# Three recurrence jobs made inside the recurrence projection; compression's gathers, weights and tables made inside the attention projection, its prompt unit first

## The chip, the cores and the metric

The kernel runs on one core of one Trainium2 chip. A core has five engines that run side by side: TensorE (PE in the profile) multiplies matrices into PSUM, VectorE (DVE) and ScalarE (ACT) do elementwise work, GpSimd (POOL) does elementwise work and issues indexed transfers, SyncE (SP) issues plain transfers. They meet by semaphores. The metric is the device time of one execution in microseconds (us); the time given is a median of runs.

## The reference, cut to what matters

One inference step of a hybrid decoder layer, for a prompt of 1024 rows and 8 sample sequences of one new row each (their 2048 past rows lie in pages). Two parts of it are touched. The first is the compression of raw keys and values, in chunks of 16 rows, for the 8 sequences (gathered by the page table) and for the prompt:

```
parts = jnp.einsum('bnsgd,rsdh->rbngh', ch, w1r)          # ch: chunks of 16 rows; r: first or second half of a block
h = parts[0, :, 0:n_cmp] + parts[1, :, 1:1 + n_cmp] + (pe.reshape(-1) @ w1) + b1
out = jax.nn.gelu(h) @ w2 + b2                            # once for keys, once for values
```

The second is a gated recurrence with 4 heads, in exact chunkwise form:

```
b = jnp.cumsum(gc, axis=2)                                # log decays
decay = jnp.exp(jnp.where(tri, b[:, :, :, None, :] - b[:, :, None, :, :], -jnp.inf))
att = jnp.einsum('bhtk,bhtsk,bhsk->bhts', qc, decay, kc)
s = jnp.exp(b_end)[..., None] * s + jnp.einsum('bhsk,bhsv->bhkv', kc * jnp.exp(b_end[:, :, None, :] - b), vc)
```

Around them stand LayerNorm and modulation, one input projection (in pieces), three attention branches, the merge, an output projection and a convolutional feed-forward. All products are float32, many as three passes over high and low parts.

## The kernel before, in words

The program is a row of stages, each a block of its own with a barrier of all engines between: modulation and norm, `project_attention` (L609), `compress` (L738), `decode_attention`, `prompt_attention`, `project_hgrn` (L1804), `hgrn_and_merge` (L1965), output projection, feed-forward. The order inside a stage is written out by hand for each engine. Nothing of a later stage starts before the barrier.

`project_attention` makes 39 products (events) from five 256-column pieces of the input weights; ACT reads the even events out of PSUM and DVE the odd ones. POOL and SP have little to do in it: SP loads the last weights at L647 and then stores the raw keys and values (L654 to L665).

`compress` first loads the page table and small constants (L821 to L831) and the first-layer weights for keys (L833), makes row indices from the page table (L905, L1092), and gathers 1 MB of pages for each sequence (L854). It works in ten units: for keys and then for values, four units of two sequences and, last of the five, one prompt unit, which reloads the prompt's rows from the stored output (L852). Per unit: 32 transposes (L899; 16 for the prompt), copied out of PSUM by ACT and DVE (L1008, 512 columns a piece); a difference on POOL (L867) and one on DVE (L1112); the first layer for two halves of the hidden units, three groups of 8 products each (L947, L949, L954, of 256 columns or of 64 for the prompt), the third group with a sum of weights that POOL makes (L874); GELU; the second layer (L969 for keys, L974 for values). A float32 product leaves two records in the trace, so a group of 8 is x16. In the eight sequence units one slice of the late modulation is worked in beside: `late_rows` (L919) between the two halves, an ACT copy (L1057), and `late_back` (L926) right behind the first layer. The transposes of unit u+1 stand before the first layer of unit u. Behind the units come the transposes and scores of the selection keys (L899, L1003).

`project_hgrn` makes 54 events from nine pieces; the last two pieces (units 7 and 8, 9 events each) only give the recurrence's inputs, and DVE makes the running sums of the log decays beside them (L1962). `hgrn_and_merge` runs 9 jobs for each of 4 heads. Jobs 0 to 6 are levels of a binary splitting: DVE makes differences of log decays (L2388, L2389; job 0 has its own form on ACT, L2296 and L2297), ACT the exponential (L2304), POOL one half of the product with k (L2105) and DVE the other with q (L2401), PE the products (L2185, L2192), DVE picks them out by a mask (L2418). Job 7 is a plain exponential, job 8 the decay to the chunk's end: a DVE difference (L2393), an exponential, a POOL product. The buffers for decays and for products are rings of three, so three jobs can be ahead.

Of the kernel before, what the change touches and what calls it, by code (L numbers as in the profile page):

```python
# [16 lines left out]
ALU = mybir.AluOpType  # L17
ACT = mybir.ActivationFunctionType
AX = mybir.AxisListType
F32 = mybir.dt.float32  # L20
# [94 lines left out]
def build(nc, a, o):  # L115
# [21 lines left out]
    with ExitStack() as ctx:  # L137
# [15 lines left out]
        with ExitStack() as left:  # L153
            with ExitStack() as att:
                with ExitStack() as h:
                    m["hTh"] = sb(h, "h_hi_1", [P, KD, T])
                    m["hTl"] = sb(h, "h_lo_1", [P, KD, T])
                    m["hl"] = [m["hTl"][:, k, :] for k in range(KD)]
                    w0, wide = nc.sbuf_base + 4 * KD * 512, 2 * GD + 3 * HEADS
                    m["w_att"] = SplitWeights(nc, None, sem, "w_att", wide, (  # L160
                        nc.alloc_sbuf_tensor_at("w_att_raw", [P, 2, 4, wide], F32, offset=w0),
                        nc.alloc_sbuf_tensor_at("w_att_parts", [P, 2, 2, KD, wide], F32, offset=w0 + 4 * 8 * wide)))
                    m["pa_mm"] = sem("pa_mm_done")
                    modulation_and_norm(nc, a, o, m, PS, sem)
                    m["kv"] = sb(att, "kv", [P, NT + 1, 6 * GD + 3 * HEADS], side="right")
                    m["qT"] = sb(att, "qT", [P, 4, T], side="right")
                    m["ksT"] = sb(att, "ksT", [P, T], side="right")
                    m["kwT"] = sb(att, "kwT", [P, T], side="right")
                    m["bg"] = sb(att, "bg", [P, NT + 1, 3 * HEADS], side="right")
                    project_attention(nc, a, o, m, PS, sem)  # L170
                m["kcTp"] = sb(att, "kcTp", [P, P], side="right")
                m["vcp"] = sb(att, "vcp", [P, GD], side="right")
                with ExitStack() as dec:
                    m["kcT"] = sb(dec, "kcT", [P, NB, NCD], side="right")
                    m["vc"] = sb(dec, "vc", [P, NB, GD], side="right")
                    m["Qz"] = sb(dec, "Qz", [P, NB * 72], side="right")
                    m["Qd"] = sb(dec, "Qd", [P, NB * HEADS], side="right")
                    m["rows"] = sb(dec, "cache_rows", [P, NB], I32, side="right")
# [13 lines left out]
            with hg:  # L192
# [13 lines left out]
                m["hl"] = [m["h_low0"][:, :]] + [m["h_low"][:, k, :] for k in range(1, KD)]  # L206
                project_hgrn(nc, a, o, m, PS, sem, at, nc.alloc_sbuf_tensor_at("scan_keep", [P, P], F32, offset=low_at))
                m["hl"] = [m["h_low"][:, k, :] for k in range(KD)]
                m["nref"] = nc.alloc_sbuf_tensor_at("minus_middle", [P, HH, NT], F32, offset=low_at + 1024)
# [399 lines left out]
def project_attention(nc, a, o, m, PS, sem):  # L609
# [4 lines left out]
    even_read, odd_read, kT_done, kT_read, stored = (sem("pa_" + x) for x in ("even_read", "odd_read", "kT_done", "kT_read", "stored"))  # L614
    with ExitStack() as st:
# [14 lines left out]
        KVQ = 3 * (NT + 1)  # L630
        block = st.enter_context(nc.Block())

        @block.sync
        def _(sp):
            sp.dma_start(m["h_hi_dram"][:, :, :], m["hTh"][:, :, :]).then_inc(spilled, 16)
            sp.dma_start(m["h_lo_dram"][:, :, :], m["hTl"][:, :, :]).then_inc(spilled, 16)
            for u, (z0, cols) in enumerate(units):
                if u < 2:
                    continue
                for s in range(2):  # L640
# [7 lines left out]
                    else:  # L648
                        sp.dma_start(weights.raw[:, s, :, 0:cols], w_dram[:, 4 * s:4 * s + 4, z0:z0 + cols]).then_inc(weights.raw_in[s], 16)
            sp.wait_ge(even_read, (KVQ + 1) // 2)  # L650
# [21 lines left out]
        def _(pe):  # L672
            unit = 0
            for e in range(FIRST, NEV):
                u, left, right, rows, cols = events[e]
                if u != unit:
                    unit = u
                    weights.ready(pe, u)
                if e >= 8:
                    pe.wait_ge(odd_read if e % 2 else even_read, e // 2 - 3)  # L680
                product(pe, PS[0:rows, EVENT_BANK[e % 8], 0:cols], left, right, KD).then_inc(mm_done, 1)

            pe.wait_ge(even_read, (NEV + 1) // 2)
            pe.wait_ge(odd_read, len(events) // 2)
# [2685 lines left out]
```

## Time and profile before

| what | value |
|---|---|
| median of 3 runs (lowest, highest) | 2432.14 us (2424.17, 2436.47) |
| the profiled execution: its own time, its span | 2429.2 us, 2427.4 us |
| mean granted TensorE clock of it | 0.954 of full |
| busy PE, DVE, ACT, POOL | 92%, 40%, 28%, 29% of the span |

The profile cuts the span into 40 slices of 60.7 us. `compress` lies in slices 4 to 9 (188 to 540 us), the recurrence in slices 19 to 21 (1092 to 1216 us). The granted clock has two levels in the records, 1.0 (2.4 GHz) and 0.5 (1.2 GHz); a value between is a mean over a stretch with both. In a timeline row the columns are start, duration, engine, line, operation, out<-in with shapes, how many instructions are merged, and in brackets the idle time before them with what ended it.

### The profile page before, as it was taken

How to read it: one execution, taken by the hardware profiler on the slowest of the kernel's cores; microseconds unless marked ns; L12 is line 12 of the kernel's file. 1: busy time of each engine (PE TensorE's matmuls, PEld its weight loads, DVE VectorE, ACT ScalarE, POOL GpSimd, SP SyncE). 2: the span in 40 equal slices, each digit the busy share in tenths (PEclk: the TensorE clock that was granted, in tenths of full speed). 3: DMA queues.
4: the chain of work that ended last, by engine and by line, in shares of the span. 5: the costliest groups of instructions: out<-in, count | busy, mean ns of one | idle time of the engine just before them, and what ended most of it. 6: DMA issues, size and time to landing. Idle time of an engine off the chain costs nothing. (4 is left out here: it accounts for less than half of the span.)

```text
span 2427.4 us, 35781 instructions
## 1 busy us (share of the span) xinstructions
PE 2236.0 (92%) x14938; PEld 1973.8 (81%) x14938; DVE 962.3 (40%) x1860; ACT 675.1 (28%) x1402; POOL 713.2 (29%) x424
## 2 busy tenths in 40 slices
PE   5996999997899989996799999999999999999997
PEld 3995777863667769995798999678989899898996
DVE  5104333123566650229932035665323333223227
ACT  3102222112465641225522221233212121121213
POOL 3203222110111122205521214264424242341526
PEclk9997999976899999997899999999999999999998
DMA  6536343226200013100032130323201120110202
GB/s 245 186 122 234 120 145 130 86 90 219 112 30 30 10 43 106 53 1 8 21 90 87 53 104 19 99 72 133 67 28 53 38 68 27 53 53 27 79 18 89
DMA packets 137655, 197.00 MB, mean 81 GB/s; under 512 B 15233, under 2 KB 106299, under 8 KB 132766
## 3 DMA queue, kind: packets, MB, share of 16 engines
q1 hardware_dynamic: 129083, 150.33, 19.3%
q0 software_dynamic: 8368, 44.12, 5.2%
q8 instruction: 118, 1.93, 0.3%
q14 instruction: 42, 0.34, 0.1%
q10 hardware_dynamic: 44, 0.27, 0.0%
HBM read 172.61 MB, written 26.36 MB: 82 GB/s over the span
## 5 line engine op out<-in xcount | busy, mean ns | idle before, releaser
L3062 PE MATMUL PS<-part_hi,w_ff_hi 128*128 128x344 f32 x1024 | 329.0, 321 | 0.0
L3062 PE MATMUL PS<-part_hi,w_ff_lo 128*128 128x344 f32 x1024 | 326.9, 319 | 0.0
L3062 PE MATMUL PS<-part_lo,w_ff_hi 128*128 128x344 f32 x1024 | 326.7, 319 | 0.0
L3062 PEld LDWEIGHTS PS<-part_hi,w_ff_hi 128*128 128x128 f32 x1024 | 192.5, 188 | 5.5 <-issue 5.1
L3062 PEld LDWEIGHTS PS<-part_lo,w_ff_hi 128*128 128x128 f32 x1024 | 192.2, 188 | 0.3
L3062 PEld LDWEIGHTS PS<-part_hi,w_ff_lo 128*128 128x128 f32 x1024 | 192.4, 188 | 0.0
L3186 POOL TENSOR_TENSOR w_ff_lo<-w_raw,w_ff_hi 128x1024 fp32r<-128x1024 f32 x42 | 100.8, 2399 | 283.5 <-ACT w_ff_hi L3139 283.5
L3239 DVE TENSOR_SCALAR conv_sb<-up_sb,conv_wT 128x1024 f32<-128x1024 f32 x22 | 44.0, 1999 | 279.6 <-ACT up_dec L3153 279.6
L1696 ACT ACTIVATE scores<-scores,mins_p 128x640 f32<-128x640 f32 (+5 forms) x192 | 112.9, 590 | 121.4 <-DVE mins_p L1736 121.4
L3103 PE MATMUL PS<-w_down_hi,act_hi 128*128 128x512 f32 x352 | 139.7, 397 | 0.0
L3103 PE MATMUL PS<-w_down_lo,act_hi 128*128 128x512 f32 x352 | 138.7, 394 | 0.0
L3103 PE MATMUL PS<-w_down_hi,act_lo 128*128 128x512 f32 x352 | 138.5, 394 | 0.0
L2160 PE MATMUL PS<-h_hi,w_merge_parts 128*128 128x344 f32 x768 | 132.2, 324 | 0.0
L3263 DVE TENSOR_TENSOR y_sum<-y_sum,PS 128x512 f32<-128x512 f32 x112 | 76.2, 687 | 138.5 <-PE PS L3103 138.2
L2160 PEld LDWEIGHTS PS<-h_hi,w_merge_parts 128*128 128x128 f32 x768 | 122.8, 189 | 3.1 <-issue 3.0
L568 POOL TENSOR_TENSOR w_merge_parts<-w_merge_raw,w_merge_parts 128x1024 fp32r<-128x1024 f32 x24 | 59.6, 2509 | 204.1 <-ACT w_merge_parts L561 204.1
L580 PE MATMUL PS<-h_hi,w_hg_parts 128*128 128x344 f32 x480 | 113.8, 320 | 0.0
L3181 POOL TENSOR_TENSOR w_down_lo<-w_down_scaled,w_down_hi 128x1024 fp32r<-128x1024 f32 x22 | 53.8, 2446 | 157.6 <-ACT w_down_hi L3134 157.6
L3139 ACT ACTIVATE w_ff_hi<-w_raw 128x1024 fp32r<-128x1024 f32 x42 | 44.5, 1058 | 194.2 <-PE PS L3062 191.2
L3134 ACT ACTIVATE w_down_hi<-w_down_scaled 128x1024 fp32r<-128x1024 f32 x22 | 23.3, 1061 | 259.4 <-PE PS L3103 193.0
L580 PE MATMUL PS<-h_hi,w_merge_parts 128*128 128x344 f32 x384 | 91.1, 320 | 1.6 <-DVE part_lo L2501 1.6
L1640 PE MATMUL PS<-ident,scores 128*128 128x128 f32 x592 | 82.5, 282 | 7.3 <-ACT PT L1691 5.6
(519 smaller groups left out, 4965.5 us busy)
## 6 DMA issues: line engine op xcount, KB each, us to landing
w_or_ada<-w_ada SPq DMA_DIRECT2D x8, 2048.0 KB, 7.9
w_raw<-w_up SPq DMA_DIRECT2D x22, 512.0 KB, 4.9
w_raw<-w_gate SPq DMA_DIRECT2D x22, 512.0 KB, 4.1
w_raw<-w_down SPq DMA_DIRECT2D x22, 512.0 KB, 3.6
w_ada_sb<-w_ada SPq DMA_DIRECT2D x4, 2048.0 KB, 17.7
w_merge_raw<-w_in SPq DMA_DIRECT2D x16, 512.0 KB, 3.9
w_hg_raw<-w_in SPq DMA_DIRECT2D x14, 512.0 KB, 3.6
h_hi_rows<-h_hi SPq DMA_DIRECT2D x1, 4128.0 KB, 13.4
```

Of the source, the lines that this page charges most:

```text
L568: pool.tensor_tensor(r32(self.lo[:, u % 2, k, 0:cols]), self.raw[:, s, :, 0:cols], self.hi[:, u % 2, k, 0:cols], ALU.subtract).then_inc(se ...
L580: last = pe.matmul(out, r32(x), r32(y), start=k + i == 0, stop=k == tiles - 1 and i == 2)
L1640: last = pe.transpose(PS[:, 4 + G % 3, P * k:P * k + P], S[:, n % 2, g, at:at + P], ident[:, :])
L1696: act.activation(S[:, n % 2, g, c:c + cols], S[:, n % 2, g, c:c + cols], ACT.Exp, bias=mn[:, n % 2, x, g:g + 1], scale=-1.0, accum_out=sm[ ...
L2160: last = pe.matmul(PS[:, e % RING, 0:W3], r32(left), r32(right), start=p == 0 and k == 0, stop=p == 2 and k == KD - 1)
L3062: last = pe.matmul(PS[:, bank(e), 0:cols], r(wt[:, s, k, :]), r(ht[:, k, t0:t0 + cols]), start=k + i == 0, stop=k == KD - 1 and i == 2)
L3103: last = pe.matmul(PS[:, bank(e), :], r(at_[:, f % AR, P * t:P * t + P]), r(wt[:, f % GRP, c]), start=f == fs[0] and i == 0, stop=f == fs[ ...
L3139: act.activation(r(wgh[:, int(kind == "gate"), :, :]), raw[:, n % RAW, :].rearrange("p (k n) -> p k n", k=KD), ACT.Copy).then_inc(hi_done, 1)
L3181: pool.tensor_tensor(r(wdl[:, f % GRP, :]), wds[:, :], wdh[:, f % GRP, :], ALU.subtract).then_inc(lo_done, 1)
L3186: pool.tensor_tensor(r(l_), w, h, ALU.subtract).then_inc(lo_done, 1)
L3239: own(v.tensor_scalar(c, up[:, 0:L], taps[0], taps[3], ALU.mult, ALU.add))
L3263: v.tensor_tensor(d, d, s, ALU.add).then_inc(acc_read, 1)
```

## The change

Three edits in one. (1) `project_attention` now also issues, on SP behind its last weights, the loads of the page table, the small constants and the keys' first-layer weights; PE makes the index product and two small transposes in a spare corner of the banks of events 29 and 31; POOL clears four tiles, makes the weight sum and issues the gathers of three sequences. Buffers get fixed places for it. (2) In `compress` the prompt unit is the first of each five, and its transposes read the projected rows `kv` in SBUF (8 transposes, 4 copies of 256 columns for a group) and not a reload. `late_rows` stands before the first half of a unit (before the second in the first sequence unit of keys and of values), and `late_back` behind the second layer of the unit before. (3) `project_hgrn` makes jobs 0, 1 and 2 of the recurrence up to their products, in the shadow of its last unit; and in all four heads job 8's difference on DVE and its one exponential become eight exponentials on ACT with the chunk's last column as bias.

```
@@ project_attention
             for u in range(1, len(units)):
                 weights.low(pool, u, landed(u), units[u][1])
+            for x in ("kcTp", "vcp", "Qz", "Qd"):
+                pool.memset(m[x][:, :], 0.0)
+            pool.wait_ge(cp["w1_in0"], 16)
+            w1 = cp["w1_or_ada0"]
+            pool.tensor_tensor(cp["w1_sum"][:, :, :], w1[:, 0:8, :], w1[:, 8:16, :], ALU.add).then_inc(sum_ready, 1)
+            pool.wait_ge(idx_ready, 2)
+            pool.wait_ge(weights.lo_done, 2 * len(units))
...
+            for b in range(3):
+                if b == 1:
+                    pool.wait_ge(mm_done, ends[3])
+                pool.indirect_dma_start(cp[f"raw{b}"][:, :], None, pages, bass.IndirectOffsetOnAxis(m["rows"][:, b:b + 1], 0))\
+                    .then_inc(cp[f"raw_in{b}"], 16)
...
+                if e == IDX:
+                    pe.wait_ge(idx_ready, 1)
+                    pe.matmul(spare(e, P, 0, NB), part[:, :], ptF[:, :], start=True, stop=True)
@@ compress
+        for pr in (None,) + tuple(range(NB // 2)):
...
+            if n is None:
+                z = GD * units[u][0]
+                for q in range(2):
+                    bank_free(pe, base + q)
+                    for t in range(4):
+                        last = pe.transpose(PS[:, (base + q) % 3, P * t:P * t + P], kv[:, 4 * q + t, z:z + GD], ident[:, :])
+                    last.then_inc(tr_done, 1)
+                return
...
-                pe.wait_ge(hb_ready, n // (len(LATE) // 2) + 1)
...
-                    if hh and u in late_at:
+                    if u in late_at and hh == late_half(u):
                         late_rows(late_at.index(u))
...
-                if u in late_at:
-                    late_back(late_at.index(u))
...
                 if u:
                     layer2(u - 1)
+                if u in late_at:
+                    late_back(late_at.index(u))
@@ project_hgrn, scalar
+                        if e in (ends[LAST - 1] + 3, ends[LAST - 1] + 5):
+                            J = (e - ends[LAST - 1] - 1) // 2
+                            act.wait_ge(diff_done, J)
+                            act.activation(E[:, J, :], E[:, J, :], ACT.Exp).then_inc(exp_done, 1)
...
+                if u == LAST - 1:
+                    raw_over(act)
+                    act.wait_ge(nref_ready, 1)
+                    first_decays(act, E, lf, nref, 0).then_inc(exp_done, 1)
@@ project_hgrn, gpsimd
+            for J in range(3):
+                pool.wait_ge(exp_done, J + 1)
+                parts_over(pool)
+                pool.tensor_tensor(pair_halves(X[:, J], J)[0], pair_halves(E[:, J], J)[0], pair_halves(kk[:, 0, 0:L], J)[0], ALU.mult)\
+                    .then_inc(mul_done, 1)
@@ hgrn_and_merge, scalar
+                elif w == 8:
+                    products_done(act, J - 3)
                     for c in range(NT):
+                        n, end = P * c, P * c + P - 1
+                        last = act.activation(E[:, J % 3, n:n + P], lf[:, h, n:n + P], ACT.Exp, bias=lf[:, h, end:end + 1], scale=-1.0)
                     last.then_inc(exp_done, 1)
```

On PE, at the start of `compress` (`kv` are the projected rows, `raw` the gathered pages, `XT` the transposed chunks), before:

```order
L905 MATMUL PS<-ptF,pagepart 128x8
L907 MATMUL PS<-ident,pe_rows 128x32
L908 MATMUL PS<-ident,b_rows 128x4
L899 MATMUL PS<-ident,raw 128x128 x64
L947 MATMUL PS<-XT,w_or_ada 128x257 x8
L949 MATMUL PS<-XT,w_or_ada 128x253 x8
L954 MATMUL PS<-XT,w_sum 128x256 x8
L919 MATMUL PS<-w_or_ada,cT 32x512 x8
```

and now:

```order
L941 MATMUL PS<-ident,kv 128x128 x8
L950 MATMUL PS<-ident,raw_570 128x128 x16
L950 MATMUL PS<-ident,raw_571 128x128 x16
L991 MATMUL PS<-XT,w_or_ada_569 128x65 x8
L993 MATMUL PS<-XT,w_or_ada_569 128x63 x8
L998 MATMUL PS<-XT,w_sum 128x64 x8
```

The index product and the small transposes are gone from here, the first first-layer groups have 64 columns and not 256, and 40 transposes stand before them instead of 64.

On DVE, at the end of `project_hgrn` and the start of the recurrence (`decays` is the ring of differences, `X` that of products), before:

```order
L1943 COPY iv<-PS 8x256
L1811 UNCONDITIONAL_BRANCH
L2375 UNCONDITIONAL_BRANCH
L2433 TENSOR_SCALAR minus_middle<-q_k_logf 128x32
L2388 TENSOR_TENSOR decays<-q_k_logf 128x16x32
L2389 TENSOR_TENSOR decays<-q_k_logf 128x16x32
L2401 TENSOR_TENSOR X<-decays,q_k_logf 128x8x64
L2388 TENSOR_TENSOR decays<-q_k_logf 128x32x16
L2389 TENSOR_TENSOR decays<-q_k_logf 128x32x16
L2401 TENSOR_TENSOR X<-decays,q_k_logf 128x16x32
L2388 TENSOR_TENSOR decays<-q_k_logf 128x64x8
```

and now:

```order
L2008 COPY iv<-PS 128x256
L2041 TENSOR_TENSOR X<-decays,q_k_logf 128x8x64
L2008 COPY iv<-PS 128x256
L2041 TENSOR_TENSOR X<-decays,q_k_logf 128x16x32
L2008 COPY iv<-PS 8x256
L2041 TENSOR_TENSOR X<-decays,q_k_logf 128x32x16
L1845 UNCONDITIONAL_BRANCH
L2464 UNCONDITIONAL_BRANCH
L2474 TENSOR_TENSOR decays<-q_k_logf 128x64x8
L2475 TENSOR_TENSOR decays<-q_k_logf 128x64x8
```

Behind the barrier (the two branches) DVE now begins with job 3's difference; one multiplication of job 2 stands between the last PSUM copy and the barrier.

## Rows read from the trace of the kernel before

**Rows 1.** Stretches: busy time of each engine, clock, DMA share and GB/s.
```profile
192.00:203.00 11.00, 0.96 (x4) 0.78 (x4) 2.34 (x13) 0.00 (x0) 4.00 (x4) 0.50 0.55 193
203.00:209.00 6.00, 5.96 (x27) 5.64 (x28) 3.12 (x5) 3.59 (x6) 1.63 (x2) 0.50 1.03 415
209.00:213.00 4.00, 3.13 (x23) 2.21 (x21) 3.91 (x7) 3.17 (x6) 3.84 (x3) 0.99 1.02 396
346.00:357.00 11.00, 11.00 (x101) 10.93 (x100) 7.39 (x9) 1.58 (x5) 4.72 (x3) 1.00 0.49 180
484.00:507.00 23.00, 23.00 (x110) 23.00 (x109) 1.07 (x5) 1.25 (x4) 0.00 (x0) 0.50 0.00 1
1100.00:1200.00 100.00, 73.04 (x839) 68.46 (x838) 96.81 (x110) 51.68 (x133) 52.70 (x32) 0.74 0.04 13
```
**Rows 2.** Timeline at the start of the compression.
```profile
187.97 0.28 PE L692 MATMUL PS<-ident,kv 8*128 8x8 f32 x2
195.34 1.15 POOL L854 DMA_INDIRECT raw<-cache_cmp_k,cache_rows  x1 [48.82 <-DVE cache_rows L1092]
203.04 6.73 PE L899 MATMUL PS<-ident,raw 128*128 128x128 f32 x32 [3.72 <-DMA raw<-cache_cmp_k,cache_rows]
205.12 1.39 DVE L1008 COPY XT<-PS 64x512 f32<-64x512 f32 x2 [5.51 <-PE PS L899]
220.86 4.51 POOL L874 TENSOR_TENSOR w_sum<-w_or_ada 128x2048 f32<-128x2048 f32 x1 [6.75 <-DMA w_or_ada<-cmp_w]
221.34 4.33 PE L947 MATMUL PS<-XT,w_or_ada 128*128 128x257 f32 x16
235.08 2.40 PE L919 MATMUL PS<-w_or_ada,cT 128*32 128x512 f32 x16 [2.53 <-DVE hid_bias L1124]
```
**Rows 3.** Timeline, PE, one sequence unit of keys to the next.
```profile
256.25 3.63 PE L947 MATMUL PS<-XT,w_or_ada 128*128 128x256 f32 x16
280.08 1.06 PE L926 MATMUL PS<-groupsum,ada_rows_late 128*128 128x9 f32 x8 [0.96 <-ACT ada_rows_late L1057]
287.30 3.63 PE L947 MATMUL PS<-XT,w_or_ada 128*128 128x256 f32 x16
```
**Rows 4.** Timeline, PE, the two prompt units and around them.
```profile
346.06 1.90 PE L947 MATMUL PS<-XT,w_or_ada 128*128 128x64 f32 x16
363.05 3.64 PE L947 MATMUL PS<-XT,w_or_ada 128*128 128x257 f32 x16
454.46 5.58 PE L947 MATMUL PS<-XT,w_or_ada 128*128 128x256 f32 x16
483.69 3.62 PE L947 MATMUL PS<-XT,w_or_ada 128*128 128x64 f32 x16
507.59 4.89 PE L899 MATMUL PS<-ident,raw 128*128 128x128 f32 x32
```
**Rows 5.** Timeline of the attention projection, SP's queue and POOL.
```profile
100.88 23.10 SPq L647 DMA_DIRECT2D w_att_raw<-w_in  x32
141.77 4.75 POOL L568 TENSOR_TENSOR w_att_parts<-w_att_raw,w_att_parts 128x1024 fp32r<-128x1024 f32 x2 [23.53 <-ACT w_att_parts L561]
```
**Rows 6.** Timeline at the start of the recurrence, DVE.
```profile
1091.60 0.41 DVE L1943 COPY iv<-PS 8x256 f32<-8x256 f32 x1 [5.22 <-PE PS L580]
1092.43 0.84 DVE L2388 TENSOR_TENSOR decays<-q_k_logf 128x512 f32<-128x512 f32 x1
1108.11 1.29 DVE L2418 COPY_PREDICATED att<-levels,PS 128x1024 f32<-128x1024 int32 x1
```
**Rows 7.** Timeline at a head's end in the recurrence, DVE and ACT.
```profile
1148.43 1.94 DVE L2393 TENSOR_TENSOR decays<-q_k_logf 128x1024 f32<-128x1024 f32 x1
1150.41 1.06 ACT L2304 ACTIVATE decays<-decays 128x1024 f32<-128x1024 f32 x1 [2.49 <-DVE decays L2393]
1155.81 1.80 DVE L2401 TENSOR_TENSOR X<-decays,q_k_logf 128x512 f32<-128x512 f32 x1 [0.77 <-issue]
```
**Rows 8.** Groups by line: count, busy us, mean ns.
```profile
L2296 ACT ACTIVATE decays<-q_k_logf 128x64 f32<-128x64 f32 x32 | 10.7, 334 | 0.0
```

More of the change, by code:

```diff
@@ L747, in compress @@
     caches = [a[x][0].rearrange("n (c s) g d -> (n c) (s g d)", s=STRIDE) for x in ("cache_cmp_k", "cache_cmp_v", "cache_sel_k")]
-    loads, units = [], []
+    loads, units, items = [], [], []
+    group = 0
     for which in range(2):
-        for pr in range(NB // 2):
-            units.append((which, pr, (len(loads), len(loads) + 1)))
-            loads += [(which, 2 * pr), (which, 2 * pr + 1)]
-        units.append((which, None, (len(loads),)))
-        loads.append((which, None))
-    NU, SEL0 = len(units), len(loads)
+        for pr in (None,) + tuple(range(NB // 2)):
+            mine = []
+            for b in ((None,) if pr is None else (2 * pr, 2 * pr + 1)):
+                mine.append(len(items))
+                items.append((len(units), len(mine) - 1, None if b is None else len(loads), group))
+                group += 2 if b is None else 4
+                if b is not None:
+                    loads.append((which, b))
+            units.append((which, pr, tuple(mine)))
@@ L792, in compress @@
-        arow = sb("ada_rows_late", [P, 512])
-        late_at = [u for u in range(NU) if u % (NU // 2) != NU // 2 - 1]
+        raw = [cp[f"raw{i}"] for i in range(RING)]
+        X, wsum, m2, w2, H, peT, b1T, hb, hb0, b2k, b2v, arow = (cp[x] for x in (
+            "XT", "w1_sum", "middle", "w2", "H", "peT", "b1T", "hid_bias", "hid_bias_half", "b2k", "b2v", "ada_rows_late"))
+        wbuf = [cp["w1_or_ada0"], cp["w1_or_ada1"]]
+        late_at = [u for u in range(NU) if units[u][1] is not None]
@@ L803, in shape, with read_to @@
             return (1, NCP + 1, NCP) if units[u][1] is None else (2, CH, NCD)
-        def unit_of(n):
-            return next(u for u in range(NU) if n in units[u][2])
         def evens(u):
             return X[:, u % 2, 0], shape(u)[1] // 2
+        def read_to(it):
+            return (it[3] + (2 if it[2] is None else 4)) // 2
         def odds(u):
@@ L876, in _ @@
[L876 to L888 removed]
+            load(RING - 1)
@@ new lines, in _ @@
+            for it in items + sel:
+                u, _, n, base = it
+                if n is not None and n + RING < len(loads):
+                    pool.wait_ge(tr_done, base + 4)
+                    load(n + RING)
+                if u is not None:
+                    later_difference(it)
+                if u == FIRST[1]:
+                    pool.wait_ge(w_in[1], 16)
+                    pool.wait_ge(l1_done, 2 * (NU // 2))
+                    pool.tensor_tensor(wsum[:, :, :], wbuf[1][:, 0:8, :], wbuf[1][:, 8:16, :], ALU.add).then_inc(sum_ready, 1)
@@ L1062, in _ @@
             u = 0
-            for n in read_chunks(act, 0, even_read):
-                if u + 1 < NU and n == units[u + 1][2][-1]:
+            for k in read_chunks(act, 0, even_read):
+                if u + 1 < NU and k == units[u + 1][2][-1]:
                     gelu(u)
@@ L1154, in late @@
                                     bT[:, t0:t0 + 4, None].to_broadcast([P, 4, 9]), ALU.add).then_inc(wa_added, 1)
[L1156 to L1158 removed]
+            for k in read_chunks(v, 1, odd_read):
+                u = items[k][0]
+                if k == units[u][2][-1]:
                     if u in FIRST:
```

393 lines of the change are left out of this document (202 added, 191 removed).

## The prediction, made before the changed kernel ran

> **What bounds the kernel now.** I read the page first (PE busy 92%), then the stretches where PE is not full or its granted clock is 0.5, then the timelines of the two stages that the change touches. TensorE bounds nearly all of the kernel. Two of its holes are touched here. In the compression's first 33.1 us, from the last small transposes of the attention projection (187.97 + 0.28 = 188.25 us) to the first 257-column group (221.34), PE does only transposes. Read the releasers: the row indices come at 195 us, the pages keep PE until 203.04, and the keys' weights, 2 MB behind everything else at over 400 GB/s, land only at 220.8, where POOL's weight sum starts [rows 1, 2]. After this PE waits once more, 2.53 us, for the hidden bias [rows 2]. In the recurrence DVE is busy 96.8 of 100 us and PE 73 [rows 1]: there DVE is the bound, and what leaves DVE counts.
>
> **Compression, its start.** The dependency on transfers goes. SP issued its last attention weights between 100.88 and 124 us; the twelve new loads stand right behind, and POOL's last weights are done at 146.5 [rows 5]. Before, the whole chain from table to first gather took 7.1 us behind 188.25 [rows 2]; issued at 124 it is through by about 132, some 15 us ahead of event 29. POOL then has the clears and a sum of 4.51 us [rows 2], and gathers from about 153 us and, for the second and third, from about 164, when the values of unit 3 are free. In the first start the first pages took 7.7 us from issue (195.34 to 203.04) [rows 2]; here they have 20. I cost this part at nothing, hidden by PE's own matmuls; if that cover failed, event 29 would stand for the landing of the table, at most these 7 us. PE gets an index product and two small transposes in the middle of its stream: 0.7 us on the path.
>
> What is late next is the reading of PSUM. From the barrier (189.7) DVE has two pairs of small copies (0.8), the prompt's four half-size copies (1.39 is two copies of 512 columns; four of 256 take that or a little more: 1.4 to 1.7), the bias columns, a wait for POOL's small difference (1.3), its own small one (0.7), and then four group reads of 1.39 for the first sequence unit [rows 2]. That is 0.8 + 1.1 (first transposes) + 1.7 + 0.4 + 1.3 + 0.7 + 5.6, so the last of the 32 transposes goes at about 199. PE's first real group therefore starts at 199 and not at 221.34.
>
> **The clock decides what this group costs.** A prompt unit is six groups of 64 columns. At the full level such a group starts every 1.8 us (346.06, 1.90 long: 10.8 us in all), at the half level every 3.42 (483.69, 3.62 long: 20.5 us) [rows 4]. The records show both: full in 346 to 357, half throughout 484 to 507, where 23 us of this work never brought the clock back [rows 1]. So such a unit keeps the level that it finds. It was at 0.5 from 192 us, and came back at 209, after 6 us of transposes at 99% busy [rows 1]. In the changed kernel the transposes are paced by DVE, 28 of them in some 6.5 us where 27 records before filled 6 us, with gaps between. I take the half level, 20.5 us; full would give 9.7 back.
>
> One rule of the Trainium skill bears on it: the page "TensorE: Matmul & The Clock Gate", section "Part 4: PE-mode transpose", says that transposes do not count as busy for the clock in the way matmuls do. This trace disagrees in part: at 209 the clock rose with nothing but transposes before it [rows 1]. By the rule the half level would hold until the first 256-column groups and cost about 1 us more than my sum; the sum goes by the rows.
>
> Then the readers turn to the next unit only when the first layer is through, with GELU of the prompt unit before ACT's read: 5.2 us of transposes and 0.8: the first sequence unit's first layer starts at 199 + 20.5 + 6.0 = 225.5.
>
> **Compression, from there.** One sequence unit of keys takes 31.05 us (256.25 to 287.30), of which 0.96 is PE waiting for ACT's copy before L926 [rows 3]. `late_back` behind the second layer has this copy long finished: 30.1. Eight such are 240.8. The third has the values' prompt transposes (8, not 32) behind it: -4.2; the last two have none there: -10.4; the second layer of values is 1.25 longer in three: +3.7; the prompt's is shorter: -0.8; the values' prompt unit, at the full level as at 346, +17.0 (346.06 to 363.05) [rows 4]. Sum 246.1, so the selection's transposes start at 225.5 + 246.1 = 471.6. Before they started at 507.59 [rows 4]: 36.0 earlier. Behind them the values' second layer of a sequence unit stands in place of a prompt's: +1.6, against transposes at the full clock instead of the half one at 507: -0.8. With the 0.7 above and 1 to 2 us for the clock falling once more in the values' units: **33 us** gained. Where it comes from: the 33.1 us hole becomes 11, the waits at L926 give 7.7, that for the bias 2.5, slow ramps the rest; the prompt unit at half clock is paid before at the end and then at the start, and cancels.
>
> Moved with it: the late modulation's weights now have to be there before a unit's first half. From the second half of one unit to the first of the next there are 30.1 - 10.4 = 19.7 us, and 2 MB at the 415 GB/s of the rows need about 5 [rows 1]. The values' weights leave after the fourth unit's `late_rows` and their sum starts when the keys' first layers are through; PE has 32 transposes and two groups ahead of its use, 9 us against 4.51 [rows 2]. Both at nothing.
>
> **Recurrence.** Before, DVE finished its last copy at 1092.0, began the differences at 1092.43, and reached the first pick (job 2) at 1108.11 [rows 6]. Now it has before this pick only job 3's and job 4's differences and job 3's multiplication: 1.3 to 2.2, 1.3 to 1.7 and 0.7 (the longer ones beside POOL). The barrier comes 0.7 later, for job 2's multiplication behind the last copy. So the pick is at 1093.0 + 4.6 = 1097.7, 10.4 us earlier; the mask (0.4 MB, 1 us at the rate of [rows 1] and some latency) is loaded at the block's start. The added work in the last projection unit (DVE some 7 us, ACT 6, POOL 4, in 26 us where both read only an event of 0.4 us every 5.8) is at nothing: PE's last eight events need no bank back.
>
> Job 8: DVE loses 1.94 in each of four heads [rows 7]. But the next step is not DVE's alone. PE runs almost without a gap there, and the multiplication of the next job 0 (1155.81) waited 0.77 for ACT. ACT now has eight pieces of 128 columns; from 0.334 for 64 columns [rows 8] and 1.06 for 1024 [rows 7] a piece is about 0.38, or 0.29 from start to start: 2.4 in place of 1.06, but it starts about 2.3 earlier. That frees ACT 0.8 to 1.0 sooner. Bounds: nothing (ACT or PE binds), or 4 x 1.94 = 7.8. I take 3.6, near the ACT row. Recurrence: 10.4 + 3.6 = **14 us**.
>
> **Sum.** 33 + 14 = 47 off 2429.2 (span 2427.4 and 1.8 around it): 2382. That execution was 2.9 under the median, so on the median's scale: **2385 us**.
>
> **Rivals.**
> - The clock is at the full level when the first prompt unit starts: 9.7 more off, 2375. For it: forty transposes before it, and in 209 to 213 transposes held the level with PE 78% busy [rows 1]. Against: it falls at 192 in the records, and rose only after 6 us of nearly unbroken transposes.
> - Part of it is given back: the values' prompt unit falls to half (+9.7), ACT's eight pieces eat the job 8 gain (+3.6), the clock falls in further units (3 each): 2398, about 34 us gained. For it: 484 to 507; against: 346 to 357 held [rows 1].
> - It does not do what it says: pages or weights still late, for instance raw pages waited for at each unit, and the recurrence bound by PE at half clock (0.74 mean in 1100 to 1200 [rows 1]): the 33 us hole reopens by 25 and the 14 shrink to 6: 2425 and up, no change.
> - Slower: the clock stays at half after the prompt unit, through sequence units. A group of 256 columns at the half level lasts 5.58 instead of 3.63 [rows 3, 4], 12 us more a unit. From the fourth such unit on it eats the 47; six give 2457. Against: at 221.34 the level came back inside the first such group (4.33 long) [rows 2].
>
> **How the numbers follow.** Forecast 0.50 (2376 to 2392 by itself), first rival 0.20, second 0.22, third 0.04, fourth 0.04. The range 2367 to 2410 holds forecast and the first two, and leaves out less than 2 in 10. A measurement of this kernel can tell about 0.5% (12 us) from no change. Faster 0.92, same 0.04, slower 0.04.
>
> **What the profile after would show.** PE's first 65-column group at about 199, no wait for a transfer before it, six groups 3.4 apart; no idle before `late_back`; selection's transposes near 471; first pick of the recurrence about 5 us after its barrier; no L2393, and the head's period about 1 us shorter. A wait of PE inside the attention projection at event 29, a wait for `w_or_ada` in any unit, or heads as long as before would show a step wrong. I am wrong in all if the compression isn't at least 20 us shorter.

## The result, and the profile after

| | before | after |
|---|---|---|
| median of the runs shown | 2428.15 us (4 runs, 2423.24 to 2436.47) | 2360.03 us (4 runs, 2359.81 to 2372.51) |
| profiled execution: time, span | 2429.2, 2427.4 | 2359.81, 2357.9 |
| mean granted clock | 0.954 | 0.973 |

The ratio after to before is 0.9733 (95% interval 0.9707 to 0.9759), so 59 to 71 us less. Forecast were 2385 us and a range of 2367 to 2410. The direction was right; the time is 7 us below the range's low end. Five more runs of the same kernel, further down, gave 0.9730 (0.9711 to 0.9748). The profiled execution is the shortest of all nine (their median is 2361.74), so what follows, read from it, shows a fortunate course of the kernel.

Where the 69.5 us between the two spans lie, read from starts in the two timelines (the block of the recurrence starts with its first transfer, at 1092.28 and 1043.02):

| stretch | before | after | shorter by | forecast |
|---|---|---|---|---|
| up to the selection's first transposes | 507.59 | 458.23 | 49.4 | 36.0 |
| up to the recurrence's block | 1092.3 | 1043.0 | 49.3 | 33 |
| first pick behind that | 15.8 | 4.3 | 11.5 | 10.4 |
| first pick to the last transposes of job 8 | 105.3 | 99.4 | 5.9 | 3.6 |
| from there to the first merge-gate matmuls | 11.1 | 8.2 | 2.9 | 0 |
| all behind that | | | 0 | 0 |

First the start of the compression after, PE's timeline (columns: start, us, engine, line, operation, tiles, shapes, count, idle before and what ended it). These rows answer to [rows 2].

```profile
187.19 0.28 PE L743 MATMUL PS<-ident,kv 8*128 8x8 f32 x2
188.93 1.06 PE L941 MATMUL PS<-ident,kv 128*128 128x128 f32 x8 [1.46 <-PEq L642]
191.23 1.89 PE L950 MATMUL PS<-ident,raw 128*128 128x128 f32 x12 [0.80 <-ACT XT L1052]
195.46 1.07 PE L950 MATMUL PS<-ident,raw 128*128 128x128 f32 x8 [2.34 <-DVE XT L1052]
197.88 1.90 PE L991 MATMUL PS<-XT,w_or_ada 128*128 128x65 f32 x16
199.61 1.95 PE L993 MATMUL PS<-XT,w_or_ada 128*128 128x63 f32 x16
...
214.27 3.63 PE L991 MATMUL PS<-XT,w_or_ada 128*128 128x256 f32 x16
...
458.23 4.04 PE L950 MATMUL PS<-ident,raw 128*128 128x128 f32 x32
```

No row waits for a transfer; the longest pause, 2.34 us, waits for DVE's reading of PSUM. The first group of 65 columns is at 197.88 (199 was forecast), but the next stands 1.73 us behind it, not 3.4, and the first sequence unit begins at 214.27, not at 225.5. The last row is the start of the selection's transposes. The same in stretches (time, length, busy us and records of PE, PEld, DVE, ACT, POOL, granted clock, DMA share, GB/s), as in [rows 1]:

```profile
187.50:197.90 10.40, 5.57 (x41) 4.34 (x42) 8.17 (x21) 5.56 (x11) 4.52 (x4) 1.00 0.78 282
197.90:214.30 16.40, 14.84 (x131) 14.12 (x130) 8.97 (x19) 7.07 (x14) 6.43 (x5) 1.00 0.42 148
214.30:458.20 243.90, 237.43 (x1354) 195.36 (x1353) 71.88 (x127) 54.09 (x98) 53.61 (x29) 1.00 0.37 129
458.20:490.70 32.50, 31.97 (x210) 18.99 (x209) 12.02 (x19) 9.59 (x16) 3.77 (x4) 1.00 0.37 130
1043.00:1147.00 104.00, 79.48 (x934) 74.60 (x935) 95.03 (x116) 63.53 (x181) 59.63 (x35) 0.84 0.06 17
```

The clock is 1.00, the level of 2.4 GHz, in all of the compression, although PE is busy in only 5.57 of the first 10.4 us. In the recurrence DVE is busy 95 of 104 us, more than any other engine. DVE's first instruction there:

```profile
1043.14 0.69 DVE L2474 TENSOR_TENSOR decays<-q_k_logf 128x512 f32<-128x512 f32 x1 [0.39 <-PEq L1845]
```

One line's rows show that stage (engine, operation, count, ns least/median/most, first and last start); the first two rows are of after, and answer to [rows 6]; the third is of before:

```profile
L2501 DVE COPY_PREDICATED att<-levels,PS x24: 1285/1314/1344, 1047.3 to 1144.8; 128x1024 f32<-128x1024 int32 x24
...
L2278 PE MATMUL PS<-ident,X x32: 272/273/301, 1061.6 to 1146.7; 128*128 128x128 f32 x32
```

```profile
L2188 PE MATMUL PS<-ident,X x32: 272/273/301, 1125.2 to 1213.4; 128*128 128x128 f32 x32
```

The stage now takes 1146.7 - 1047.3 = 99.4 us from its first pick to the last transpose of job 8; before 1213.4 - 1108.1 = 105.3. Of job 8, DVE's row of [rows 7] is gone, and ACT has this:

```profile
1140.87 2.45 ACT L2388 ACTIVATE decays<-q_k_logf 128x128 f32<-128x128 f32 x8
```

### The profile page after: what moved, and what is told of

It reads as the page before. It is cut to its first block and busy times, and to the rows that moved or that the text cites. A ratio compares the mean times of both kernels' runs of the same rounds, so it can differ in the third digit from the quotient of the medians.

```text
span 2357.9 us, 35773 instructions
## 1 busy us (share of the span) xinstructions
PE 2198.3 (93%) x14922; PEld 1939.2 (82%) x14922; DVE 946.0 (40%) x1851; ACT 681.5 (29%) x1430; POOL 712.3 (30%) x426
## 6 DMA issues: line engine op xcount, KB each, us to landing
w_ada_sb<-w_ada SPq DMA_DIRECT2D x4, 2048.0 KB, 17.7
```

## The experiments

The theory: the sum failed above all in the clock level of the first prompt unit, and the rest is in terms of the gain that were sized too low. The rivals: the early loads alone make the gain and the order of units is worth nothing; or the recurrence's part is worth more than the sum gave it. All runs are told. Differences between kernels are of medians, or of rows where a row is named.

**c_only and r_only: the two parts apart.** The first has the recurrence's functions of before in the changed kernel, the second the reverse.

```
# c_only: build, project_hgrn, hgrn_and_merge as before; all else changed
# r_only: build's E, X, nref, hp; project_hgrn, hgrn_and_merge changed; all else as before
```

> The changed kernel with the recurrence as it was before; the compression, its early gathers and its order of units stay changed. Theory: the two parts don't touch each other, and the compression alone is worth what stands at the start of the recurrence's block in the two profiles, 49.3 us: 2428 - 49 = 2379 us, first 65-column group near 197.9 us, six groups 1.8 us apart, first 256-column group near 214.3. Rival (the sizes of the prediction): 33 us, so 2395, groups 3.4 us apart. Second rival: part of the 49 us is chance of one execution; then the ratio is between 0.980 and 0.986.

> The kernel before with the recurrence part of the change alone. Theory: 20.2 us minus up to 3 us that the last head's end gained by a shorter store of the state (3.5 instead of 5.1 us) and a higher clock, so 17 to 20 us: 2408 to 2411. Rival (the prediction's size): 14 us, 2414. First pick about 4.3 us after the block's start in both.

c_only: 2387.87 us, ratio 0.9828 (0.9809 to 0.9846), 37 to 46 us less. r_only: 2411.74 us, ratio 0.9937 (0.9925 to 0.9950), 12 to 18 less. Together 57 us, of 68. But c_only's profiled execution shows what its size depends on (stretches, as above):

```profile
196.00:199.00 3.00, 1.60 (x12) 1.30 (x12) 2.91 (x5) 1.19 (x2) 0.82 (x2) 0.97 1.02 412
199.00:226.00 27.00, 26.46 (x131) 25.47 (x130) 9.34 (x20) 7.27 (x14) 7.13 (x5) 0.56 0.29 100
```

Here the clock did fall, in the last transposes, and the six groups stand 3.4 us apart as forecast: from the first (199.96) to the first sequence unit (226.37) it is 26.41 us. In the changed kernel's profile the same way took 16.39. So the compression's gain is as large as the theory has it, less these 10 us in this execution. c_only's five times go from 2380.8 to 2392.1: its lowest is 47 us under the median of before. The 11 us that the two parts together lack against the whole fit the 10 us of the half level.

r_only: first pick at 1092.5 and last transposes of job 8 at 1191.6, 99.1 us, as in the changed kernel. From pick and heads it gains 11.5 + 6.2 = 17.7 in the profile; the median shows 16.5. The forecast of 14 lies in its interval too.

```profile
L2471 DVE COPY_PREDICATED att<-levels,PS x24: 1287/1314/1352, 1092.5 to 1189.7; 128x1024 f32<-128x1024 int32 x24
...
L2248 PE MATMUL PS<-ident,X x32: 272/273/301, 1106.7 to 1191.6; 128*128 128x128 f32 x32
```

From those transposes to the merge gate r_only has 11.1 us and c_only 8.3. So the 2.9 us of that stretch don't come from the recurrence's change. In part they are DVE's wait for the store of the state, of which these are the rows of before and after:

```profile
1219.82 0.29 DVE L2427 COPY state<-PS 128x128 f32<-128x128 f32 x1 [5.14 <-DMA out_hgrn_p<-state]
```

```profile
1151.54 0.29 DVE L2510 COPY state<-PS 128x128 f32<-128x128 f32 x1 [3.51 <-DMA out_hgrn_p<-state]
```

This wait is 5.14 and 5.09 us in the two kernels without the compression's part (before, r_only) and 3.51 to 3.72 in the profiles of all eleven others that have it in this place, prompt_last too. So its 1.5 us come with the early loads or the fixed places of buffers, and not from one execution to the next; how is not shown. The rest is PE's clock: where the first merge-gate group is at half (3.6 us long and not 2.8), the stretch is 1.3 us longer.

**job8_dve: the difference of job 8 back on DVE.**

```
# exponential(), ACT: taken out
-                elif w == 8:
-                    products_done(act, J - 3)
...
# diff(), DVE: difference of 1024 columns; then ACT's one exponential
+                if w == 8:
...
+                    v.tensor_tensor(e3, b3[:, :, P - 1:P].to_broadcast([P, NT, P]), b3, ALU.subtract).then_inc(diff_done, 1)
```

> The changed kernel with job 8's difference back on DVE in all four heads and one exponential of 1024 columns; the three jobs made ahead stay. Theory: DVE is the bound of the recurrence and job 8 is worth 1.5 us a head, so the last job-8 transposes stand 108.8 us behind the block's start instead of 102.9, and the time is 2366. Rival (the prediction): ACT or PE binds next and it is worth 3.6 us in all: 106.5 us and 2364. Upper bound 4 x 1.94 = 7.8 us: 2368.

```profile
L2499 DVE COPY_PREDICATED att<-levels,PS x24: 1285/1308/1352, 1053.0 to 1154.5; 128x1024 f32<-128x1024 int32 x24
...
L2278 PE MATMUL PS<-ident,X x32: 272/273/421, 1069.5 to 1157.6; 128*128 128x128 f32 x32
```

From the first pick to the last transposes of job 8 it is 1157.6 - 1053.0 = 104.6 us, 5.2 more than after. Job 8 is worth 5.2 and not 3.6, read from one profile each; theory near, forecast too low. PE's waits show the way: ahead of the four heads' job-8 transposes it waits 8.1 us in all for POOL's product before and in job8_dve, 2.2 after and in r_only. The time, 2372.05 us, ratio 0.9770 (0.9748 to 0.9793), is 9 to 12 us over the changed kernel's; the surplus is not in this stage: between the two profiles 3.6 us lie ahead of the selection, 2.1 between it and the recurrence, 1.3 ahead of the merge gate.

**late_back_first and late_as_before: the places of the late modulation.** The forecast laid the end of the 0.96 us waits [rows 3] to the new place of `late_back`. The first kernel moves that back, the second `late_rows` as well.

```
                 layer1(u)
+                if u in late_at:
+                    late_back(late_at.index(u))
                 if u:
                     layer2(u - 1)
-                if u in late_at:
-                    late_back(late_at.index(u))
# late_as_before also: def late_half(u): return 1
```

> The changed kernel with late_back directly behind the first layer, ahead of the second layer of the unit before, as it was. Theory: PE waits about 0.96 us for ACT's copy in each of eight sequence units as before, 7.7 us: 2368, with the wait in front of late_back's matmuls. Rival: with late_rows ahead of the unit's first half the copy is finished in time anyway, wait 0: 2360. The profile's waits before late_back's line decide.

> The changed kernel with both places of the late modulation as before: late_rows ahead of the second half of a unit, late_back directly behind its first layer. Theory: with late_rows only 10 us ahead, and ACT's copy behind its other work, the waits of before return, 9.3 us in eight units (18.6 with the weight loads counted too): 2368. Rival: late_rows' place means little and late_back's place with it (2.3 us in all): 2363.

late_back_first: 2365.04 us, 0.9747 (0.9727 to 0.9767), not to be told from the changed kernel. late_as_before: 2385.13 us, 0.9819 (0.9804 to 0.9834). What the waits are, by that line's view (first after, then late_back_first, then late_as_before; before has the same 18.6 in 16):

```profile
  ACT ada_rows_late L1108: 2.1, 4
```

```profile
  ACT ada_rows_late L1108: 4.6, 4
```

```profile
  ACT ada_rows_late L1108: 18.6, 16
```

The two numbers are us and times. This view adds the waits of the matmuls and of their weight loads, which overlap; the expectation's 9.3 us was half of its 18.6. In PE's own rows the wait is 0.96 us in each of eight units before and in late_as_before (7.7 us); in late_back_first it is 0.96 in two units (1.9), and after 0.57 and 0.36 (0.9). Both times these are the two units whose `late_rows` stands where it did. So most of the waits went, as forecast, but not all. With `late_rows` ahead of the first half, 10 us earlier, `late_back`'s new place has only 1.0 us left to take. `late_back`'s place alone, with `late_rows` as before, wasn't run, so what it would give by itself is not shown.

late_as_before is 22 us slower than the changed kernel on the same chip (2363.43), far more than these waits. Its profiled execution, the lowest of five (2379.27; the others are near 2385), is 19.5 us longer than after's: 11.8 us up to the selection (the waits; one group of 256 columns at 5.36 us in a fall of the clock in the values; a later start), 6.0 from the selection to the recurrence's block, where the kernels don't differ, and 1.7 behind. In the fourteen profiles of this case that stretch between varies from 584.0 to 590.8 us (before 584.7, after 584.8). The rest of the 22 us stays open.

**pages_late and pages_late_busy: what the early gathers hide.**

```
# project_attention, POOL: the three indirect_dma_start taken out
-            load(RING - 1)
+            for n in range(RING):
+                load(n)
# pages_late_busy also, on PE behind the prompt's transposes:
+            for _ in range(16):
+                pe.matmul(PS[:, 6, 0:256], ident[:, :], kv[:, 0, 0:256], start=True, stop=True)
```

> The changed kernel with the first three gathers issued at the compression's start instead of inside the attention projection; table, small inputs, keys' weights, their sum and the order of units stay early. Theory: PE has the prompt's 8 transposes and is then idle some 6 us until the pages land near 197.5; the granted clock falls to half, the prompt unit's six groups are 3.4 us apart, and the first 256-column group starts about 7 + 10 = 17 us later than 214.3, near 231: 2377 us. Rival: the pause costs only itself and the clock holds: groups 1.8 us apart, near 221, 2367.

> As pages_late, with 16 matmuls of 256 columns (about 7 us, result not used) on PE behind the prompt's transposes, so that it works while the pages are on their way. Theory (the clock at the first prompt unit is set by what PE did before it): the clock stays full, groups 1.8 us apart, the first 256-column group near 221 to 222, 2367 to 2368. Rival (the level in this place has another cause): groups 3.4 us apart and the same time as pages_late, 2377.

pages_late: 2371.59 us, 0.9762 (0.9747 to 0.9778); pages_late_busy: 2370.33 us, 0.9762 (0.9749 to 0.9775). The timelines, first pages_late:

```profile
200.16 4.78 PE L945 MATMUL PS<-ident,raw 128*128 128x128 f32 x24 [8.83 <-DMA raw<-cache_cmp_k,cache_rows]
...
206.13 1.90 PE L986 MATMUL PS<-XT,w_or_ada 128*128 128x65 f32 x16
```

```profile
185.69 7.07 PE L1018 MATMUL PS<-kv,ident 128*128 128x256 f32 x32
194.84 1.53 PE L945 MATMUL PS<-ident,raw 128*128 128x128 f32 x12 [2.08 <-DMA raw<-cache_cmp_k,cache_rows]
```

The gathers hide about 7 us: the first group is 8.25 us later than after, 1.3 of them from the stage before. The theory for the clock failed here: PE was idle 8.83 us and the clock fell at 193, but it was back in the middle of the transposes (at 203), before the first group. With PE busy it never fell (1.00 in each us from 188 to 208). The times don't tell the two kernels apart: four of pages_late_busy's five are near 2370 and the profiled one is the fifth, 2363.05, so what the others had is not seen.

**prompt_last: the order of units.** Early gathers, early weights and their sum stay; the bias columns and the exception for `late_rows` move to the unit that is now first.

```
-        for pr in (None,) + tuple(range(NB // 2)):
+        for pr in tuple(range(NB // 2)) + (None,):
```

> The changed kernel with the prompt unit last in keys and values as before; early gathers, early weights and their sum, and late_back behind the second layer stay. Theory: the order is worth the half-clock prompt unit at the end of the values (9.7 us) and the wait for the hidden bias (2.5 us): 2372, with six groups 3.4 us apart at the end. Rival: the early loads alone make the gain and the order is worth nothing: 2360 to 2363.

2377.42 us, 0.9785 (0.9761 to 0.9809), 14 to 17 us over the changed kernel's two medians. PE's timeline:

```profile
203.20 3.65 PE L950 MATMUL PS<-ident,raw 128*128 128x128 f32 x16 [5.60 <-DVE XT L1052]
206.64 4.41 PE L991 MATMUL PS<-XT,w_or_ada 128*128 128x257 f32 x16
...
451.80 1.98 PE L991 MATMUL PS<-XT,w_or_ada 128*128 128x64 f32 x16
453.62 3.31 PE L993 MATMUL PS<-XT,w_or_ada 128*128 128x62 f32 x16
456.71 3.62 PE L998 MATMUL PS<-XT,w_sum 128*128 128x64 f32 x16
```

The rival that the early loads do it all falls. A sequence unit put first can't begin before 206.64, since PE waits 5.60 us for the readers of its pages; and at the end the values' prompt unit falls to half, as in [rows 4], here behind its first group and with PE not idle. Its selection starts at 473.78, 15.6 us later than 458.23. The order is worth about 15 us in these two profiles; the expectation had the half-clock unit at the end, but not the readers at the start. The wait of 2.53 us for the hidden bias [rows 2], which it had in the order too, is absent here: it went with what is made early. The values' prompt unit runs at half in all three profiles that have it last (before, r_only, prompt_last) and at full in the eleven others, where it stands in the middle.

**readers_first: DVE's order at the start, and the store's wait.**

```
+                if k == 0:
+                    continue
+                if k == 1:
+                    bias_columns(0)
+                    first_difference(0)
# state(): the wait on `stored` moved from chunk 0 to chunk 1
```

> The changed kernel with two small moves: DVE reads the first sequence unit's first pages before it takes the prompt unit's difference (for which it waits on POOL), and in the recurrence the wait for the stored state stands before the second chunk of a head instead of the first. Theory: PE's 2.3 us idle before the prompt unit is DVE's order, and goes; first 65-column group near 196, and 0.9 us less at the last head's end: 2357. Rival: reading PSUM itself paces the 40 transposes and the group stays at 197.9: 2359 to 2360. The timing can't tell these apart, the profile can.

2371.17 us, 0.9767 (0.9753 to 0.9780). The theory fell. PE's timeline:

```profile
184.85 1.07 PE L941 MATMUL PS<-ident,kv 128*128 128x128 f32 x8 [1.46 <-PEq L642]
...
193.75 3.68 PE L991 MATMUL PS<-XT,w_or_ada 128*128 128x65 f32 x16 [1.77 <-DVE XT L1144]
```

After has it alone, readers_first beside POOL's:

```profile
193.20 0.69 DVE L1144 TENSOR_TENSOR XT<-XT 128x512 f32<-128x512 f32 x1 [1.16 <-POOL XT L913]
```

```profile
190.85 2.84 DVE L1144 TENSOR_TENSOR XT<-XT 128x512 f32<-128x512 f32 x1
```

```profile
190.82 2.33 POOL L913 TENSOR_TENSOR XT<-XT 128x1008 f32<-128x1008 f32 x1 [0.55 <-DVE XT L1052]
```

From the first transposes to the first group it is 8.90 us, against 8.95 after. The small difference, 0.69 us in the profile after, now ran beside POOL's and took 2.84, which ate the gain, and the idle time only moved to a place directly ahead of the group, where the clock fell. The other half of the edit worked: from the recurrence's block to the merge gate it is 111.2 us against 111.9 after, 0.7 of the 0.9 expected.

**after_again, held and pause_first: the clock of the first prompt unit.** The first is the changed kernel unaltered. The others:

```
# held, PE, between the first sequence unit's two pages:
+                        if k == 2:
+                            for _ in range(5):
+                                pe.matmul(PS[:, 6, 0:256], ident[:, :], kv[:, 0, 0:256], start=True, stop=True)
# pause_first, SP behind the last of the 40 transposes, and PE ahead of the first group:
+            for x in range(3):
+                sp.dma_start(m2[:, 0, x:x + 1], a["c_chunkpart"][:, :]).then_inc(pause, 16)
+                sp.wait_ge(pause, 16 * (x + 1))
+                if u == 0:
+                    pe.wait_ge(pause, 48)
```

> The changed kernel once more, with nothing altered, beside the three that follow. Theory (the first prompt unit of keys runs at full or at half clock from execution to execution): the executions spread over two levels about 10 us apart, near 2360 and near 2370, and the profiled one shows the level of its six groups: 1.8 us apart with the first 256-column group 16.4 us behind the first group, or 3.4 us apart and 26.4 us. Rival (the changed kernel is always at full clock there): all within 3 us of 2360, and the one execution at 2372.5 has another cause.

> The changed kernel with 5 matmuls of 256 columns (2.2 us in all, result not used) on PE between the transposes of the first sequence unit's first and second pages, where it waited 2.34 us. Theory: with PE at work there the clock does not fall before the prompt unit, all executions stand at the lower level, near 2360, and the profile has no second at 0.50 before 216 us. Rival: the fall isn't tied to this pause, and some executions are 10 us longer as before.

> The changed kernel with PE held for three short DMAs, one after the other (about 6 us), between the last of the 40 transposes and the prompt unit's first group. Theory: the clock falls in the pause and groups of 64 columns don't bring it back: six groups 3.4 us apart, 6 + 10 = 16 us longer than the changed kernel at full clock, 2376, in every execution. Rival: the groups are matmuls and raise the clock within a few us, so it costs the pause and 2 to 4 us: 2368 to 2370.

On one chip: after_again 2363.43 us (2369.26, 2369.19, 2361.74, 2361.05, 2363.43), held 2360.92 (2359.33 to 2364.53), pause_first 2385.28 (2379.78 to 2388.14). after_again was profiled in its longest execution:

```profile
194.80 1.06 PE L950 MATMUL PS<-ident,raw 128*128 128x128 f32 x8 [2.35 <-DVE XT L1052]
196.13 1.70 PE L950 MATMUL PS<-ident,raw 128*128 128x128 f32 x8 [0.27 <-DVE XT L1052]
197.63 3.51 PE L991 MATMUL PS<-XT,w_or_ada 128*128 128x65 f32 x16
200.94 3.62 PE L993 MATMUL PS<-XT,w_or_ada 128*128 128x63 f32 x16
...
224.04 2.33 PE L991 MATMUL PS<-XT,w_or_ada 128*128 128x256 f32 x10
```

The same kernel, the same waits to 0.02 us, the same pause, and this time the clock fell. So the level is not a property of the kernel. In stretches:

```profile
196.00:197.60 1.60, 1.47 (x8) 1.31 (x9) 1.46 (x3) 1.25 (x3) 1.37 (x1) 0.65 1.05 411
197.60:224.00 26.40, 25.86 (x130) 24.92 (x129) 8.86 (x18) 7.01 (x13) 6.55 (x5) 0.57 0.26 88
```

It costs 26.41 - 16.39 = 10.0 us here, and the whole span is 9.5 us longer (2367.4 against 2357.9). So the kernel has two courses. Of its nine timed executions six lie at 2359.8 to 2363.4 and three at 2369.2 to 2372.5; for two, one of each kind, a profile shows the level. For the other seven it is inferred from the time; their mean granted clocks (0.968 to 0.973 in the first kind, 0.965 to 0.969 in the second) overlap. held fills the pause:

```profile
194.38 2.32 PE L1027 MATMUL PS<-kv,ident 128*128 128x256 f32 x10
196.89 1.06 PE L950 MATMUL PS<-ident,raw 128*128 128x128 f32 x8 [0.19 <-DVE XT L1055]
```

Its clock is 1.00 throughout, it costs nothing (8.94 us from first transposes to first group), and none of its five executions is at the upper level. It has the lowest ratio of all, 0.9721 (0.9705 to 0.9737), but by intervals it can't be told from the changed kernel. With six of nine at the lower level, five in a row at it would come by chance about once in eight times (an estimate, 6/9 to the fifth power), so that the filling prevents the fall is not shown. pause_first asks whether groups of 64 columns bring the clock back:

```profile
208.17 3.68 PE L998 MATMUL PS<-XT,w_or_ada 128*128 128x65 f32 x16 [9.54 <-DMA middle<-c_chunkpart]
```

```profile
202.00:208.00 6.00, 0.00 (x0) 0.00 (x0) 1.22 (x1) 0.00 (x0) 1.61 (x1) 0.50 0.42 157
208.00:235.00 27.00, 26.33 (x129) 25.54 (x130) 5.00 (x14) 6.38 (x12) 1.57 (x2) 0.55 0.26 83
```

The clock fell in a pause of 9.54 us directly ahead of the group (longer than the 6 meant), and the six groups never raised it: first group to first sequence unit is 26.68 us. 9.5 + 10 us is near the 22 us by which its median stands over after_again. The rival, that groups bring the clock back, falls.

## Why the prediction was wrong, and where it was right

By its own steps. Between the two profiles the shortfall of the sum is 69.5 - 47 = 22.5 us. Another 2.9 us are the scale: they were added because the profiled execution lay under a median of three; over four runs that median is 2428.15, 1 us below it.

- **"I take the half level, 20.5 us": the step that failed, 10.1 us.** The price was right: at half level first group to first sequence unit took 26.41 us in two executions against the forecast of 20.5 + 6.0. The level was a choice between two courses that this kernel really has, and the commoner one, six of nine executions by their times, was put at a chance of 0.20 as the first rival. The prediction saw that transposes raised the clock and that 64-column groups did not, and took from [rows 1] that it falls at 192 here too. But there PE had been busy for 0.96 of 11 us; with a pause of 2.34 us the clock falls only in some executions, and may be raised again by the transposes behind it, as in job8_dve.
- **That is not all of it.** An execution at the half level is 2369, still 16 us under 2385. Most other terms were sized on the same side:
- First group at 199: measured 197.88, 1.1 us better. 0.8 of the 1.1 is that the attention projection ended at 187.47 instead of 188.25. Whether its additions cost nothing can't be read from that: it ends at 182.46 in r_only, whose projection is unaltered, and at 183.3 to 189.1 in the changed kernels. PE waits for none of the additions.
- 246.1 us from the first sequence unit to the selection: 244.0. The period of a unit with 32 transposes, forecast 30.1, is 29.92 (246.16 to 276.08). The size was right, the cause only partly: `late_rows` has a share, as late_as_before shows, and "no idle before `late_back`" holds for six units of eight.
- The values' weights and the modulation's at nothing: right, PE waits for none.
- 3 us taken off behind the selection's start for the second layer, small additions and more falls of the clock: 0.1 measured. In this execution the clock never fell in 184 to 490 us. That is luck in part: in four of the other changed kernels' profiles (job8_dve, late_as_before, pause_first, readers_first) it fell once for 3.4 us between 435 and 458, the 1 to 2 us that the prediction set aside.
- Recurrence, first pick: 10.4 forecast, 11.5 measured; the pick stands 4.3 us behind the barrier, 4.6 was summed.
- Job 8: 3.6 forecast, 5.9 between the two profiles and 5.2 by job8_dve. The point that ACT's row sets it was too cautious: two thirds of the upper bound of 7.8 came, since POOL's product, and PE's transposes behind it, came earlier by more than the ACT row gave (0.52 us of waiting after, 1.69 before, in the last head).
- The last head's end at nothing, without a reason: 2.9 us. 1.5 of it, the shorter store, goes with the compression's part in every profile; about 1.3 is PE's clock, which differs from profile to profile and is luck.

Added: 10.1 + 1.1 + 2.1 + 2.9 + 1.1 + 2.3 + 2.9 = 22.5.

The second rival (part given back) and the third (loads still late) did not happen in the profile after; the fourth (half clock through sequence units) is excluded: in all four profiles with the half level in the first prompt unit (c_only, after_again, readers_first, pause_first) the first group of 256 columns is at full (3.63 us). The page "TensorE: Matmul & The Clock Gate" of the Trainium skill, section "Part 4: PE-mode transpose", by which transposes don't count as busy in the way matmuls do, is not borne out here: in pages_late the clock rose at 203 with nothing but 3 us of transposes before it, after 8.83 us of idle time.

What a better sum would have been: the two levels weighed by how much PE idles before (2.34 us in one pause, against 0.96 us busy in 11 before the change), and on the scale of the larger median. With the sum's other terms that is 2381 at half and 2371 at full, still above the result, by the terms that were rounded to the safe side.

## What to carry to other kernels

A stage of small matmuls that finds TensorE's clock at half stays there: no group of 64 columns brought it back here, in seven such stretches in seven profiles. At full it mostly stays at full, but not surely (prompt_last lost it behind the first group). Such a stage costs 10.8 us here at one level and 20.5 at the other, so its place in the program matters: at the end of the values it was the dearer one in three profiles of three. Where a level of the clock decides a term, look for two groups of execution times before calling one of them the result. Filling a known pause of TensorE with throwaway matmuls cost nothing here (held) and may help; that it does is not shown. And when five small terms are each rounded to the safe side, their sum isn't a central forecast.

## What the hardware showed unexpectedly

- The same code up to this place, with the same pause of 2.34 to 2.36 us on PE, went three ways: no fall of the clock (after), a fall at 196 that transposes undid by 200 (job8_dve, late_back_first, late_as_before), a fall at 196 to 199 that then held for 24 us (after_again, c_only).
- PE idle for 8.83 us lost the clock, and 3 us of transposes (200.16 to 203) won it back; six groups of 64 columns, 20 us without a gap, did not; in after_again it came back at 220, in the 16 transposes behind them (218.00 to 221.35).
- Two elementwise operations on the same tile, one on DVE and one on POOL: the DVE difference of 512 columns took 0.69 us alone and 2.84 us beside POOL's of 1008 columns.
